# A feed-forward down projection in seven block products instead of eight, with its weight and activation sums on VectorE

## What is computed

```python
        x = x + merged @ w_out[l]
        h2 = rms_norm(x, g_ffn[l])
        x = x + jnp.square(jax.nn.relu(h2 @ w_ff1[l])) @ w_ff2[l]
```

## Time and profile before

| what | value |
|---|---|
| median of 3 runs | 704.57 us (704.14 to 705.61) |
| profiled execution | 704.41 us, of which the span of the profile is 702.6 us |
| TensorE busy | 695.7 us, 3338 matmuls |
| VectorE, ScalarE, GpSimd busy | 392.5, 310.1, 327.9 us |
| granted TensorE clock | 1.00 |

### The profile page before, as it was taken

One profiled execution on the slowest core, in us unless ns is written; L12 is line 12 of the kernel. 1 busy time (PEld: TensorE's weight loads), 2 busy tenths in 40 slices (PEclk: granted clock), 3 DMA queues, 4 the chain that ended last, 5 costly groups with the idle time before them and its releaser, 6 DMA issues.

```text
span 702.6 us, 9265 instructions
## 1 busy us (share of the span) xinstructions
PE 695.7 (99%) x3338; PEld 572.8 (82%) x3338; DVE 392.5 (56%) x553; ACT 310.1 (44%) x572; POOL 327.9 (47%) x201
## 2 busy tenths in 40 slices
PE   9999999999999999999999999999999999999998
PEld 7878788888888888878888888888888888888887
DVE  6775798555555556867866411454115541255796
ACT  7755676666665666533443221333213331133310
POOL 1366566455555562434444444444444444444442
PEclk9999999999999999999999999999999999999999
DMA  8222142222222124432332332223222232222331
GB/s 308 90 91 90 50 133 90 77 76 91 91 90 90 62 61 122 150 119 91 110 100 90 101 109 90 90 90 112 97 90 90 94 115 90 90 90 90 109 101 61
DMA packets 22910, 69.89 MB, mean 99 GB/s; under 512 B 2731, under 2 KB 4267, under 8 KB 22876
## 3 DMA queue, kind: packets, MB, share of 16 engines
q1 hardware_dynamic: 22588, 68.92, 30.0%
q10 hardware_dynamic: 288, 0.52, 0.2%
HBM read 67.27 MB, written 2.16 MB: 99 GB/s over the span
## 4 chain that ended last, share of the span: by engine, by line
PE 88%; issue 6%; POOL 2%; DVE 2%; ACT 1%; DMA 1%; SPq 0%; POOLq 0%; DVEq 0%; ACTq 0%
PE bank L885 27%; PE bank L887 26%; PE bank L886 26%; POOL w_lo L324 2%; PE bank L1016 2%; PE bank L1029 2%; PE bank L1049 1%; PE bank L1051 1%; DVE store L628 1%; DMA store<-x_t 1%; PE bank L969 0%; PE bank L911 0%; PE bank L974 0%; PE bank L912 0%; PE bank L963 0%
## 5 line engine op out<-in xcount | busy, mean ns | idle before, releaser
L324 POOL TENSOR_TENSOR w_lo<-w_raw,w_hi 128x1024 fp32r<-128x1024 f32 x111 | 267.6, 2411 | 301.2 <-ACT w_hi L378 301.2
L885 PE MATMUL bank<-x_hi,w_hi 128*128 128x512 f32 (+1 forms) x592 | 233.8, 395 | 0.9 <-POOL w_lo L324 0.9
L887 PE MATMUL bank<-x_hi,w_lo 128*128 128x512 f32 (+1 forms) x592 | 229.1, 387 | 0.0
L886 PE MATMUL bank<-x_lo,w_hi 128*128 128x512 f32 (+1 forms) x592 | 229.0, 387 | 0.0
L378 ACT ACTIVATE w_hi<-w_raw 128x1024 fp32r<-128x1024 f32 x112 | 118.4, 1057 | 163.2 <-PE bank L887 163.2
L885 PEld LDWEIGHTS bank<-x_hi,w_hi 128*128 128x128 f32 x592 | 111.2, 188 | 29.3 <-issue 4.4
L887 PEld LDWEIGHTS bank<-x_hi,w_lo 128*128 128x128 f32 x592 | 111.2, 188 | 23.2
L886 PEld LDWEIGHTS bank<-x_lo,w_hi 128*128 128x128 f32 x592 | 111.3, 188 | 21.4 <-issue 0.2
L885 PE MATMUL bank<-qk_hi,w_hi 128*128 128x512 f32 x320 | 125.2, 391 | 0.0
L887 PE MATMUL bank<-qk_hi,w_lo 128*128 128x512 f32 x320 | 124.5, 389 | 0.0
L886 PE MATMUL bank<-qk_lo,w_hi 128*128 128x512 f32 x320 | 124.5, 389 | 0.0
(11 more groups left out here) (106 smaller groups left out, 641.8 us busy)
## 6 DMA issues: line engine op xcount, KB each, us to landing
w_raw<-slabs SPq DMA_DIRECT2D x112, 512.0 KB, 3.3
store<-x_t SPq DMA_DIRECT2D x16, 256.0 KB, 3.9
bias_m<-tab_dram SPq DMA_DIRECT2D x8, 256.0 KB, 4.3
out<-store SPq DMA_DIRECT2D x7, 256.0 KB, 2.2
bias_m<-tab_dram SPq DMA_DIRECT2D x8, 128.0 KB, 4.4
w_raw<-slabs ACTq DMA_DIRECT2D x1, 384.0 KB, 4.0
w_raw<-slabs SPq DMA_DIRECT2D x1, 384.0 KB, 6.2
out<-store SPq DMA_DIRECT2D x2, 128.0 KB, 1.7
```

The costliest lines, as they stand in the source:

```text
L324: pool.tensor_tensor(w_lo[:, g % WS, :], w_raw[:, g % RAW, :], w_hi[:, g % WS, :].bitcast(F32), ALU.subtract).then_inc(w_lo_ready, lots)
L885: pe.matmul(out_, wh, xh, start=first, stop=False)
L886: pe.matmul(out_, wh, xl, start=False, stop=False)
L887: last = pe.matmul(out_, wl, xh, start=False, stop=end)
```

## The change

**The down projection in seven products.** The feed-forward is now 8 chunks (`CHUNKS`) of 512 hidden features. In a chunk, 4 up slabs (`TILES`) give four tiles of activations, and 4 loads of 128x1024 give a 512x1024 piece of `w_ff2` as four blocks B11, B12, B21, B22 of 256x512. The activations are split likewise into blocks of 256 features by 256 tokens (`a11` to `a22`). The product of two such 2x2 block matrices is made from seven block products instead of eight, of sums of blocks: `t_1 = B12 - B11`, `t_2 = B22 - t_1`, then `B22 - B12` and `B21 - t_2` on the weights; `s_3`, `a21 + a22`, `s_2`, `s_4` on the activations. The sums are made in float32, and then each of the seven weight units and seven activation parts is split into high and low. The activation is now the stationary operand, and the output is token-major. A block product is 12 matmuls of 128x512: two halves `m` of the tokens, two of the contraction `p`, three of precision.

**Who does what in a chunk.** VectorE has four weight sums, the low parts of the units 1, 2, 4 and 6 (`down_lo`), the low parts of the chunk's four up slabs (`up_lo`), four activation sums, seven activation low parts (`u_part_lo`) and 14 additions from banks (`add_product`). GpSimd has the low parts of units 0, 3 and 5, those that are blocks as loaded. ScalarE has the seven high parts of units (`down_hi`), four slabs' high parts, relu and now also the square, and seven high parts of activations. `weight_sums` stands at the start of VectorE's chunk, behind the additions of the chunk before.

**Bounds of the chunk.** TensorE does up slabs 1 to 4 and then products 0 to 6; slab 4 is the first of the next chunk, so it stands between a chunk's last activations and its first product. The last chunk has no slab 4. Blocks are loaded ahead: B11 again after product 2, B12 after product 4, B22 and B21 after product 5. Seven chunks are turns of a loop, the last is written out.

**x, the norm, the output.** In the output projection TensorE transposes every tile of the new x (`x1_transpose`, four 128x128 each, eight tiles) and ScalarE copies the rows. GpSimd clears the eight sums. The mean square comes from four squares of rows on ScalarE with an accumulator; they stand between the first up slab and the first chunk, and VectorE waits for them ahead of its first chunk. The matmuls with ones, the sums of squares and the split of the last slab are gone. In the last chunk VectorE does eight sums `sum * r2 + x` ahead of its activations, and the products come in by three-operand operations.

On VectorE, the loop of the feed-forward in the kernel before. The first rows are of the up slabs (`probs` are the squared activations), the last ones of the down slabs.

The diff, cut to its core:

```diff
-CHUNKS = 4
-PER_CHUNK = 16
+CHUNKS, TILES = 8, 4
+BANK_OF = [X_BANK, Z_BANK, Y_BANK, X_BANK, Z_BANK, Y_BANK, Z_BANK]
+READ_LAST = [3, 6, 5, 0, 1, 2, 4]
+FREED_BY = [4, 5, 6, 3, 0, 1, 2]
+U_ORDER = [0, 4, 1, 2, 3, 5, 6]
+T_UNITS, B_UNITS = (1, 2, 4, 6), (0, 3, 5)
...
+            def chunk_lows(c):          # GpSimd
+                for k in B_UNITS:
+                    down_lo(k, c)
...
+            def chunk(c, last=False):   # ScalarE
+                down_hi(0, c)
+                down_hi(1, c)
+                down_hi(2, c)
+                relu(1, c)
+                split_hi(G_FF + 3, c)
+                square(1, c)
+                down_hi(3, c)
+                relu(2, c)
+                if not last:
+                    split_hi(G_FF + 4, c)
+                square(2, c)
+                u_part_hi(0, c)
+                u_part_hi(4, c)
+                relu(3, c)
...
+            relu(0, 0)
+            split_hi(G_FF + 2)
+            square(0, 0)
+            x1_rows_copy(KT - 1)
+            act.wait_ge(x1_rows_ready, KT)
+            for t in range(QT):
+                if t:
+                    act.wait_ge(ms2_ready, t)
+                act.activation(flat(u_raw[:, 2:4, :]), x1_rows[:, t, :], ACT.Square,
+                               accum_out=ms2[:, t:t + 1]).then_inc(ms2_ready, 1)
...
+            def weight_sums(c):         # VectorE
+                dve.tensor_tensor(t_1, raw_b[B12], raw_b[B11], ALU.subtract).then_inc(t_ready, 1)
+                dve.tensor_tensor(t_2, raw_b[B22], t_1, ALU.subtract).then_inc(t_ready, 1)
+                down_lo(1, c)
+                down_lo(2, c)
+                dve.tensor_tensor(raw_b[B12], raw_b[B22], raw_b[B12], ALU.subtract).then_inc(t_ready, 1)
+                dve.tensor_tensor(t_2, raw_b[B21], t_2, ALU.subtract).then_inc(t_ready, 1)
+                up_lo(3, c)
...
+            dve.wait_ge(ms2_ready, QT)
...
+            with dve.Fori(0, CHUNKS - 1) as c:
+                weight_sums(c)
+                u_sums(c)
+                add_products(c)
...
+                for m in range(2):      # TensorE, product(k, c)
+                    if final and k == 6:
+                        pe.wait_ge(out_ready, 3 + m)
+                    else:
+                        pe.wait_ge(sum_read, product_count(back, m, c) - (2 * PRODUCTS if back >= k else 0))
+                    for p in range(2):
+                        pe.matmul(out_, u_high, high[:, p, :], start=(k in OPENS and p == 0), stop=False, ...)
+                        pe.matmul(out_, u_high, low[:, p, :], start=False, stop=False, ...)
+                        last = pe.matmul(out_, u_low, high[:, p, :], start=False, stop=(p == 1), ...)
...
             with pe.Fori(0, CHUNKS - 1) as c:
-                feed_forward(c)
-            pe.wait_ge(x1sum_ready, N_OUT - 1)
-            mean_square(r_all[:, :], bank[6]).then_inc(ms2_done, 1)
-            feed_forward(CHUNKS - 1, True)
+                for j in range(1, TILES + 1):
+                    up(j, c)
+                for k in range(PRODUCTS):
+                    product(k, c)
```

More of the change, by code:

```diff
@@ L79, in sb, with two @@
             return ctx.enter_context(nc.sbuf_tensor(name, shape, dt))
+        def two(name, shape):
+            at = nc.sbuf_base
+            first = sb(name, shape, R)
+            return first, nc.alloc_sbuf_tensor_at(name + "_again", shape, F32, offset=at)
         def sem(name):
@@ L306, in _ @@
-            for n in range(KT - 1):
-                sp.wait_ge(out_ready, n + 1)
[L308 to L312, removed]
+                if G_OUT + 5 <= g < G_OUT + 9:
+                    if g == G_OUT + 5:
+                        sp.wait_ge(max_ready, 2 * STEPS)
+                        sp.wait_ge(slab_done, G_OUT)
+                    b = (B11, B12, B22, B21)[g - G_OUT - 5]
+                    load_down(b, slabs[G_DOWN + b])
@@ L314, in _ @@
+            with sp.Fori(0, CHUNKS - 2) as c:
+                loads(c, range(AHEAD, AHEAD + TILES))
+            loads(CHUNKS - 2, [AHEAD])
+            for n, (j, m) in enumerate((j, m) for j in (0, 3, 1, 2) for m in range(2)):
+                sp.wait_ge(out_ready, n + 1)
+                sp.dma_start(out[tokens(j, m)][:, S * (j % 2):S * (j % 2 + 1)], sums[j][m]).then_inc(out_stored, 16)
+            sp.wait_ge(out_stored, 16 * 8)
         @block.gpsimd
@@ L563, in _, with relu @@
-            act.wait_ge(x1sum_ready, N_OUT - 1)
-            with act.Fori(0, CHUNKS - 1) as c:
[L565 to L572, removed]
+                if n:
+                    x1_rows_copy(n - 1)
+            def relu(j, c):
+                act.wait_ge(slab_done, c * TILES + (G_FF + j + 1))
+                act.activation(u_raw[:, j % TILES, :], bank[7 - j % 2][:, :], ACT.Relu).then_inc(relu_ready, 1)
@@ L574, in _ @@
+            chunk(CHUNKS - 1, True)
         @block.vector
@@ L851, in _ @@
[L851 to L876, removed]
@@ new lines, in _ @@
+            c = CHUNKS - 1
+            weight_sums(c)
+            dve.wait_ge(sum_read, product_count(0, -1, c))
+            dve.wait_ge(r2_ready, 2)
+            for j in range(4):
+                for m in range(2):
+                    t = tokens(j, m)
+                    dve.scalar_tensor_tensor(out=sums[j][m], in0=sums[j][m], scalar=r2[:, t:t + 1], in1=x1_part(j, m),
+                                             op0=ALU.mult, op1=ALU.add).then_inc(rest_sum_ready, 1)
+            u_sums(c, True)
@@ L1139, in out_part, with x1_transpose @@
                     last.then_inc(slab_done, 1)
+            def x1_transpose(n):
+                pe.wait_ge(acc_read, read(G_OUT + n))
+                if n >= 5:
+                    pe.wait_ge(x1_rows_ready, n - 4)
+                for t in range(QT):
+                    last = pe.transpose(bank[n % 5][:, P * t:P * t + P], store[:, n, P * t:P * t + P], ident[:, :])
+                    if (n, t) == (N_OUT - 2, 0):
+                        last.then_inc(product_done, 2 * PRODUCTS)
+                last.then_inc(x1t_done, 1)
             out_part(0, range(KT - 1))
@@ new lines, in product @@
+            def product(k, c, final=False):
+                if k in T_UNITS:
+                    pe.wait_ge(t_lo_ready, c * 4 + (T_UNITS.index(k) + 1))
+                else:
+                    pe.wait_ge(b_lo_ready, c * 3 + (B_UNITS.index(k) + 1))
+                pe.wait_ge(u_lo_ready, u_count(k, c))
+                high, low = (halves(of[SLOT[k]]) for of in (unit_hi, unit_lo))
+                for m in range(2):
+                    back = READ_LAST[k]
+                    if final and k == 6:
+                        pe.wait_ge(out_ready, 3 + m)
+                    else:
+                        pe.wait_ge(sum_read, product_count(back, m, c) - (2 * PRODUCTS if back >= k else 0))
+                    out_ = bank[BANK_OF[k] + m][:, :]
+                    for p in range(2):
+                        at = slice(S // 2 * p + P * m, S // 2 * p + P * m + P)
+                        u_high, u_low = x_hi[:, k, at], x_lo[:, k, at]
+                        pe.matmul(out_, u_high, high[:, p, :], start=(k in OPENS and p == 0), stop=False,
+                                  skip_group_check=True)
+                        pe.matmul(out_, u_high, low[:, p, :], start=False, stop=False, skip_group_check=True)
+                        last = pe.matmul(out_, u_low, high[:, p, :], start=False, stop=(p == 1),
+                                         skip_group_check=True)
+                    last.then_inc(product_done, 1)
@@ L1184, in rel_bucket @@
+            for k in range(PRODUCTS):
+                product(k, CHUNKS - 1, True)
 def rel_bucket(n):
```

343 lines of the change are left out of this document (249 added, 94 removed).

## The result

| | before | changed |
|---|---|---|
| median | 704.66 us (704.14 to 705.61, 4 runs) | 712.68 us (712.29 to 714.03, 4 runs) |
| profiled execution | 704.41 us, span 702.6 us | 712.88 us, span 711.0 us |

The changed kernel takes 1.0119 times as long, with a 95% interval of 1.0107 to 1.0131. It is slower, 8.0 us by the medians and 8.4 by the spans of the two profiled executions. The forecast was +8.6, 713.0 us.

The account below looks back on a forecast made before the run. TensorE, busy 99%, was taken to bound the kernel. Terms -19.2 + 10.6 + 10.4 + 1.7 + 3.9 + 1.2 = +8.6 on 704.4 gave 713.0 us; main case 708 to 718, whole range 700.5 to 721.

Parts of the forecast that it names:

- The matmuls: TensorE's work: fewer matmuls in the second projection, mean square and last slab, less added transposes, sum -19.2 us.
- the rival on the pace: Matmuls with activations as weights keep another pace than 0.2266 us, 0.7 us for each nanosecond; given little chance.
- A group of transposes: Four transposes of x in the output projection cost TensorE 0.47 us, eight groups +3.8.
- The steady wait: Third up slab of six middle chunks and the last waits 1.52 us, GpSimd issued ahead of VectorE's up_lo(3): +10.6.
- VectorE wins the race: Steady chunk: up_lo(3) goes ahead of GpSimd, the 1.52 us waits vanish, 702.4 us (699 to 705); chance 0.22.
- turn of the loop: VectorE's loop turn is costly, six turns of 1.5 us add 9: 722 us; chance 0.17, shared with a slower VectorE.
- The first wait: First chunk: weight sums wait for four row squares, so TensorE idles 10.4 us before the third up slab.
- The clock: Behind the first chunk's long idling, eight matmuls go slow, 0.2 us more each: +1.7.
- The last chunk: No fourth up slab as cover; products 0, 1 and 6 wait 0.9, 1.4 and 1.6 us for VectorE: +3.9.
- product 6: Last chunk: it waits 1.6 us for product 4's bank, behind VectorE's 20 sums and two low parts.
- The end behind the last matmul: VectorE ends 1.8 us behind TensorE instead of 1.1, and the last transfer is 256 KB instead of 128 KB: +1.2.

Follow-up runs that it names:

- experiment 2: Changed kernel with VectorE's w_lo of the third up slab moved ahead of the last two weight sums: 697.75 us, 0.9909.
- experiment 1: Changed kernel, ScalarE's high part of unit 3 moved: first kernel, behind relu(2), 702.37 us; second, right behind unit 2's high part, 712.77 us.
- experiment 3: Changed kernel with the first chunk written out, its weight sums ahead of the clearing, row squares and factors moved to the last chunk: 705.30 us, 1.0015.
- experiment 5: Changed kernel with TensorE's first chunk written out and 42 filler matmuls ahead of its third up slab: 710.73 us, 1.0090.
- experiment 4: Changed kernel with w_lo ahead of the last two weight sums, first chunk's weight sums ahead, and row squares in the last chunk: 691.01 us, 0.9806.
- second kernel of experiment 6: Kernel with both the w_lo and first-chunk edits, the last chunk's eight three-operand sums done for one column of 512 only: 686.78 us, 0.9749.

## Why the prediction was right

**The matmuls.** The turns without a wait in experiment 2 take 40.80 for 180 matmuls, 0.2267 each for activations as the stationary operand too, so the rival on the pace is out. A group of transposes costs what was forecast: the last matmul ahead of one starts at 352.06, the second behind it at 352.96 instead of 352.51, 0.45, and 0.47 to 0.49 with the next few. Removed and added matmuls make -20.5 for -19.2. The kernel before wasn't at full pace everywhere: its first slab of the output projection waits for `w_lo` (a gap of 1.26 ahead of 316.50), and the first group of transposes now falls into that wait; and it loses 0.19 once in each chunk (at 397.63, 484.85, 572.09 and 660.22), which the prediction took for nothing.

**The steady wait.** The step was right, engine by engine. With 454.32 as time 0, `t_1` starts at 0.81 (forecast 0.81), GpSimd is issued at 8.74 (8.75), `w_lo` at 9.04 (8.98) and ends at 12.46 (12.40). The size was a little off: 12.6 for the seven, where 10.6 was written. Left out were the 0.13 from `w_lo`'s end to TensorE's first matmul and 0.10 in the pace right behind a wait. The rival *VectorE wins the race* needed 0.23 us and had 0.30 against it; experiment 1 shows that its price was right, 10.8 for six waits where 10.6 was written for seven. The rival *turn of the loop* is out by the rows above: 454.52 to 455.13 is 0.61, the pitch of two operations without a loop.

**The first wait.** Forecast 10.4, found 10.5. Of its cause experiments 2 and 3 show both parts: what stands ahead of the weight sums (10.5 to 3.0) and the length of the chain (10.5 to 6.2). The prediction names the squares alone. They did come last, and `t_1` starts 13.57 after the first up slab (forecast 13.55), but GpSimd's and VectorE's clearing, which it doesn't mention, ends only 1.55 earlier.

**The clock.** Forecast 1.7, found 1.65: eight distances of 3.46 together for 1.81. That there would be slow matmuls was right; that it was eight is in part luck, since behind the same wait there are 7 in the first kernel of experiment 1 and 14 in its second (1.5 and 2.9 us). The rule of the Trainium skill (TensorE: Matmul & The Clock Gate, Part 1) that activity releases a throttled default is borne out by the rows with 0.52 and by experiment 5.

**The last chunk.** Here a step failed. Products 0 and 1 wait 1.0 and 1.3 (forecast 0.9 and 1.4), but product 6 doesn't wait at all, where 1.6 was forecast. The 1.6 doesn't follow from the 20 sums and two low parts that the prediction names: they take 15.6 (692.82 to 708.44), less than the 17.9 of products. It would need a hold-up of VectorE by some 2 us. The race that could give one, GpSimd's low part of unit 5 against VectorE's of unit 4, isn't named there, and VectorE was first:

```profile
694.68 1.22 DVE L1034 TENSOR_TENSOR v_parts<-bias_m,v_parts 128x1024 fp32r<-128x1024 f32 x1
694.84 3.33 POOL L495 TENSOR_TENSOR pt_hi<-qk_hi_again,v_parts 128x1024 fp32r<-128x1024 f32 x1 [15.98 <-ACT v_parts L706]
```

VectorE is 0.16 ahead and runs through; GpSimd takes 3.33 instead of 2.4, and nobody waits for it. VectorE has read product 4's first bank at 703.8, and product 6 starts at 704.32. What the other order would have cost here wasn't tried. The end behind the last matmul is 711.0 - 707.04 = 4.0 for 3.2 before, +0.8 where 1.2 was written, since VectorE is 1.4 behind instead of 1.8.

**The sum.** -20.5 + 12.6 + 10.5 + 1.65 + 2.3 + 0.8 = +7.4, and 0.3 more in the gaps behind the waits. From the last transposes of the attention (122.82 before, 123.40 after) to the end of the span the difference is 7.8. The other 0.6 of the spans' 8.4 lies ahead of them, where the edit changes nothing; in all ten profiles these transposes stand between 122.39 and 123.94, so of a difference between two spans up to 1.5 us can come from there. The forecast's 8.6 is so near because misses of +2.0 in the steady waits, -1.6 in product 6 and -1.3 in the matmuls, with the smaller ones, nearly cancel. That is luck. Read as terms the forecast is right to about 2 us, not to 0.2.

## What to carry to other kernels

Cost a change that trades TensorE's work for VectorE's by VectorE's order around the first thing that TensorE needs, not by its busy share: at 76% busy in a chunk it cost 1.8 us of wait each turn because two sums that nobody needed yet stood first. Where VectorE and GpSimd both read two SBUF operands, the one issued first went first in every meeting read here, by 0.18, 0.30 and 0.34 for GpSimd and by 0.16 for VectorE, so a forecast needs both issue times, and a margin of a few tenths has to be kept as a case of its own. Work put between a prologue and a loop (here two clearings and four row squares) is paid for if the loop's first step waits for it; look where its result is used.

## What the runs showed of the hardware

Behind every wait of TensorE of 2.7 us and more the clock was lower in these kernels; I had expected that for the long one only. With 42 fillers nothing fell. The waits of 1.7 in the feed-forward never did it in any kernel. In the kernel's first microseconds one was followed by it, in the changed kernel: TensorE idles 1.65 until 6.76, and then the clock falls though it works (the columns are those of the table of stretches above).

```profile
4.50:7.90 3.40, 1.61 (x9) 1.10 (x8) 1.67 (x4) 2.42 (x5) 0.00 (x0) 1.00 1.00 352
7.90:11.30 3.40, 3.40 (x9) 2.56 (x9) 3.40 (x6) 3.40 (x6) 0.00 (x0) 0.50 1.01 376
```

After 3.0 idle us (experiment 3) the granted clock was 0.52 for 3.5 us. In experiment 2 a wait of 3.3 ahead of product 0 was followed by six matmuls at full pace and only then by slow ones, 0.43 apart and more; the granted clock is 1.00 from 672.70 to 674.10 and 0.50 from 674.10 to 677.50:

```profile
672.71 0.47 PE L1455 MATMUL bank<-v_parts,x_hi 128*128 128x512 f32 x1 [3.11 <-issue]
673.02 0.39 PE L1457 MATMUL bank<-v_parts,x_hi 128*128 128x512 f32 x1
...
674.17 0.63 PE L1455 MATMUL bank<-v_parts,x_hi 128*128 128x512 f32 x1
674.60 0.63 PE L1457 MATMUL bank<-v_parts,x_hi 128*128 128x512 f32 x1
675.02 0.63 PE L1458 MATMUL bank<-v_parts,x_lo 128*128 128x512 f32 x1
```

So the price of such a wait can come late. By the distances it is 1.5 to 2.9 us of TensorE's time in the nine cases of these profiles, and the longest wait isn't the dearest: 1.65 behind 10.5 in the changed kernel, 2.9 behind 3.8 in experiment 4. In the last chunk, where VectorE is the bound, little of it reaches the end: in experiment 4 VectorE waits 0.9 for banks behind the slow matmuls, and for none in the second kernel of experiment 6, where the clock doesn't fall. Before the change TensorE's longest idle time in the trace is 1.3 us.
